# Layer norms with running moments, and four weight strips side by side, in a two-block transformer kernel on one NeuronCore

## What is computed

```
h = LN1(ALPHA*x + 0.5*swiglu(x))                       # FFN1, down projection, norm 1
h = LN2(ALPHA*h + token_mixers(h @ w_in) @ w_out)      # norm 2
h = LN3(ALPHA*h + cross_attention(h, LN(mem)))         # norm 3
h = LN4(ALPHA*h + 0.5*swiglu(h))                       # FFN2, down projection, norm 4
hm = rms_norm(h)*(1 + scale) + shift                   # "MODN": modulated input of block two
out = h + gate * merge(neighbourhood_attention(hm), short_conv(hm), conformer(hm))
_layer_norm(x): mu = mean(x); var = mean((x - mu)**2); (x - mu)*rsqrt(var + 1e-5)*g + b
```

## Time and profile before

| | us |
|---|---|
| median of 3 runs (lowest, highest) | 1776.18 (1774.76, 1776.67) |
| profiled execution, its own time | 1776.79 |
| its span | 1775.2 |
| TensorE busy | 1729.3 |
| VectorE busy | 964.0 |
| ScalarE busy | 678.1 |
| GpSimd busy | 167.3 |

### The profile page before, as it was taken

How to read it: one execution, slowest core, us unless ns; L and a number is a source line. 1 busy time by engine, 2 the same in 40 slices (tenths; PEclk the granted TensorE clock), 3 DMA queues, 4 the chain that set the end, 5 groups by cost and what they waited for, 6 DMA issues and landing times.

```text
span 1775.2 us, 22509 instructions
## 1 busy us (share of the span) xinstructions
PE 1729.3 (97%) x8312; PEld 1396.7 (79%) x8312; DVE 964.0 (54%) x1244; ACT 678.1 (38%) x945; POOL 167.3 (9%) x163
## 2 busy tenths in 40 slices
PE   8999999989999999999999999998999999999999
PEld 6888888857787778886888888865777777788887
DVE  4333339876964654546333333336968768744442
ACT  4232232244435455535322322235454544733321
POOL 0000001121013501012000000003010120000000
PEclk9999999999999999999999999998999999999999
DMA  5222247623222334122322323321222222133231
GB/s 207 95 95 95 95 139 244 210 70 126 73 72 75 104 131 154 60 83 72 106 95 99 101 95 107 107 83 54 84 94 92 88 86 83 59 127 111 100 104 69
DMA packets 50460, 183.74 MB, mean 104 GB/s; under 512 B 5664, under 2 KB 5920, under 8 KB 50016
## 3 DMA queue, kind: packets, MB, share of 16 engines
q1 hardware_dynamic: 44352, 161.50, 27.2%
q10 hardware_dynamic: 5040, 16.00, 2.6%
q0 software_dynamic: 1008, 5.41, 0.9%
HBM read 180.79 MB, written 2.10 MB: 103 GB/s over the span
## 4 chain that ended last, share of the span: by engine, by line
PE 89%; DVE 7%; ACT 2%; issue 1%; DMA 0%; DVEq 0%; ACTq 0%
PE proj L362 80%; PE aux L465 3%; DVE w_lo L354 1%; PE aux L1333 1%; DVE y L1487 1%; DVE a_lo L504 1%; PE aux L1320 1%; DVE h L500 1%; PE aux L1125 1%; ACT w_hi L347 1%; PE proj L1146 1%; PE aux L1310 0%; DVE score L764 0%; PE aux L1313 0%; DVE md L790 0%
## 5 line engine op out<-in xcount | busy, mean ns | idle before, releaser
L354 DVE TENSOR_TENSOR w_lo<-raw,w_hi 128x1024 fp32r<-128x1024 f32 x304 | 390.6, 1286 | 443.4 <-ACT w_hi L347 436.3
L362 PE MATMUL proj<-a_hi,w_hi 128*128 128x512 f32 x1504 | 598.3, 398 | 20.0 <-DVE a_lo L504 10.4
L362 PE MATMUL proj<-a_lo,w_hi 128*128 128x512 f32 x1504 | 589.1, 392 | 0.0
L362 PE MATMUL proj<-a_hi,w_lo 128*128 128x512 f32 x1504 | 589.1, 392 | 0.0
L347 ACT ACTIVATE w_hi<-raw 128x1024 fp32r<-128x1024 f32 x304 | 319.6, 1053 | 266.9 <-PE proj L362 243.3
L362 PEld LDWEIGHTS proj<-a_hi,w_hi 128*128 128x128 f32 x1504 | 284.5, 189 | 87.0 <-issue 26.2
L362 PEld LDWEIGHTS proj<-a_lo,w_hi 128*128 128x128 f32 x1504 | 284.6, 189 | 60.4 <-issue 2.6
L362 PEld LDWEIGHTS proj<-a_hi,w_lo 128*128 128x128 f32 x1504 | 284.3, 189 | 59.8
L362 PE MATMUL proj<-hid_hi,w_lo 128*128 128x512 f32 x352 | 137.1, 390 | 0.0
L362 PE MATMUL proj<-hid_lo,w_hi 128*128 128x512 f32 x352 | 137.1, 389 | 0.0
L362 PE MATMUL proj<-hid_hi,w_hi 128*128 128x512 f32 x352 | 137.1, 389 | 0.0
(11 more groups left out here) (296 smaller groups left out, 1941.3 us busy)
## 6 DMA issues: line engine op xcount, KB each, us to landing
raw<-stream SPq DMA_DIRECT2D x304, 512.0 KB, 3.5
ctxk<-ada_in ACTq DMA_DIRECT2D x12, 512.0 KB, 3.6
ctxv<-ada_in ACTq DMA_DIRECT2D x12, 512.0 KB, 4.2
h<-x_in SPq DMA_DIRECT2D x4, 512.0 KB, 6.9
out<-h ACTq DMA_DIRECT2D x8, 256.0 KB, 2.0
btab<-rpb_in POOLq DMA_DIRECT2D x4, 384.0 KB, 3.5
cond_row<-cond_in ACTq DMA_DIRECT2D x1, 1024.0 KB, 7.5
side<-mem_in POOLq DMA_DIRECT2D x1, 1024.0 KB, 5.1
```

Of the source, the lines that this page charges most:

```text
L354: nc.vector.tensor_tensor(w_lo[:, st.slot], raw[:, st.slot], w_hi[:, st.slot].bitcast(F32), ALU.subtract).then_inc(lo_ready, 1)
L362: mm = nc.tensor.matmul(dst, a, b, start=start and n == 0, stop=stop and n == 2)
```

## The change

Three things are edited.

First, norms 1, 3 and 4 get running moments. After the residual of chunk 4, TensorE makes the mean over the first four chunks (`pe_mid`, with a matrix of 1/512), and VectorE subtracts it from all 8 chunks (`dve_shift`), those not yet complete included. From then on ScalarE squares each complete chunk and VectorE adds the squares (`act_square`, `dve_add_square`) between the splits of the last strips. At the end four mean matmuls follow (`pe_moments`: sum, squares, last chunk, last square), ScalarE squares the mean, VectorE takes it from the mean square (`dve_variance`), and the remaining mean is subtracted chunk by chunk within `dve_normalise` (`dve_recentre`).

Second, norm 2 keeps its form, but VectorE adds its squares (`dve_add_squares`), so that one mean matmul stands where eight stood, and the order of splits around it is changed.

Third, `strip_quad` takes the place of `strip_pair` at the start of the mixer, of FFN2 and of the first round of the attention: four strips side by side for 5 of the 8 chunks, then each strip's last three chunks. The fourth strip's split is moved ahead for this. The loops over the residual projections of these norms are written out.

```
+        QUAD_BESIDE = 5
+        def strip_quad(pe, st, g, ready):
+            four = [(st.plus(j), g.plus(j)) for j in range(RING)]
+            for k in range(QUAD_BESIDE):
+                ready(k)
+                for s, gg in four:
+                    if k == 0:
+                        pe.wait_ge(lo_ready, s.n + 1)
+                        ge(pe, proj_read[gg.slot], gg.turn)
+                    product(proj[:, gg.slot], w_hi[:, s.slot, k * P:(k + 1) * P], w_lo[:, s.slot, k * P:(k + 1) * P],
+                            a_hi[:, k], a_lo[:, k], k == 0, False)
+            for s, gg in four:
+                for k in range(QUAD_BESIDE, KD):
+                    if s is four[0][0]:
+                        ready(k)
+                    mm = product(proj[:, gg.slot], w_hi[:, s.slot, k * P:(k + 1) * P],
+                                 w_lo[:, s.slot, k * P:(k + 1) * P], a_hi[:, k], a_lo[:, k], False, k == KD - 1)
+                mm.then_inc(strip_done, 1)
...
+        def residual_done(eng, m, c):
+            eng.wait_ge(proj_read[m.groups[c].slot], m.groups[c].turn + 1)
+        def pool_running(pool, m):
+            for c in (1, 2, 3):
+                residual_done(pool, m, c)
+                if c == 1:
+                    residual_done(pool, m, 0)
+                else:
+                    pool.wait_ge(r_sum, 5 * m.r + c - 1)
+                nc.gpsimd.tensor_tensor(zsum, h[:, 0] if c == 1 else zsum, h[:, c], ALU.add).then_inc(r_sum, 1)
+            pool.wait_ge(r_mid, m.r + 1)
+            for c in (5, 6):
+                residual_done(pool, m, c)
+                if c == 5:
+                    pool.wait_ge(r_shift, 8 * m.r + 5)
+                else:
+                    pool.wait_ge(r_sum, 5 * m.r + 4)
+                nc.gpsimd.tensor_tensor(zsum, h[:, 4] if c == 5 else zsum, h[:, c], ALU.add).then_inc(r_sum, 1)
+        def pe_mid(pe, m):
+            pe.wait_ge(r_sum, 5 * m.r + 3)
+            ge(pe, r_shift, 8 * m.r)
+            nc.tensor.matmul(aux[:, 2], mean_w[:], zsum, start=True, stop=True).then_inc(r_mid, 1)
+        def pe_moments(pe, m, beside=None):
+            pe.wait_ge(r_sum, 5 * m.r + 5)
+            ge(pe, r_cent, 8 * m.r)
+            nc.tensor.matmul(aux[:, 0], mean_d[:], zsum, start=True, stop=False)
+            pe.wait_ge(r_acc, 6 * m.r + 6)
+            nc.tensor.matmul(aux[:, 1], mean_d[:], rstd, start=True, stop=False)
+            if beside:
+                beside()
+            residual_done(pe, m, KD - 1)
+            nc.tensor.matmul(aux[:, 0], mean_d[:], h[:, KD - 1], start=False, stop=True).then_inc(r_mean, 1)
+            pe.wait_ge(r_sq, 9 * m.r + KD)
+            nc.tensor.matmul(aux[:, 1], mean_d[:], sq[:, 1], start=False, stop=True).then_inc(r_ms, 1)
+        def dve_shift(dve, m):
+            dve.wait_ge(r_mid, m.r + 1)
+            for c in range(KD):
+                if c == 4:
+                    residual_done(dve, m, 4)
+                nc.vector.tensor_tensor(h[:, c], h[:, c], aux[:, 2], ALU.subtract).then_inc(r_shift, 1)
+        def act_square(act, m, c):
+            if c == 0:
+                nc.scalar.preload_act_table_set(LN_EXP)
+            if c <= 4:
+                act.wait_ge(r_shift, 8 * m.r + c + 1)
+            else:
+                residual_done(act, m, c)
+            if c >= 2:
+                act.wait_ge(r_acc, 6 * m.r + max(1, c - 2))
+            nc.scalar.activation(sq[:, c % 2], h[:, c], ACT.Square).then_inc(r_sq, 1)
+        def dve_add_square(dve, m, c):
+            dve.wait_ge(r_sq, 9 * m.r + c + 1)
+            if c > 1:
+                dve.wait_ge(r_acc, 6 * m.r + c - 1)
+            nc.vector.tensor_tensor(rstd, sq[:, 0] if c == 1 else rstd, sq[:, c % 2], ALU.add).then_inc(r_acc, 1)
+        def dve_residual_of(dve, m, c, st, factor):
+            g = m.groups[c]
+            res = result(dve, st, g)
+            if c >= 5:
+                dve.wait_ge(r_shift, 8 * m.r + c + 1)
+            nc.vector.scalar_tensor_tensor(h[:, c], res, factor, h[:, c], ALU.mult,
+                                           ALU.add).then_inc(proj_read[g.slot], 1)
+        def dve_recentre(dve, m, c):
+            if c == KD - 1:
+                dve.wait_ge(r_sq, 9 * m.r + KD)
+            nc.vector.tensor_tensor(h[:, c], h[:, c], aux[:, 0], ALU.subtract).then_inc(r_cent, 1)
+        def act_mean_square(act, m):
+            act.wait_ge(r_mean, m.r + 1)
+            act.wait_ge(r_acc, 6 * m.r + 6)
+            nc.scalar.activation(sq[:, 0], aux[:, 0], ACT.Square).then_inc(r_sq, 1)
+        def act_running_std(act, m, chain):
+            act.wait_ge(r_var, m.r + 1)
+            inverse_root(chain, rstd, rstd, m.eps).then_inc(n_std, 1)
+        def dve_variance(dve, m, beside=None):
+            dve.wait_ge(r_sq, 9 * m.r + KD + 1)
+            dve.wait_ge(r_ms, m.r + 1)
+            nc.vector.tensor_tensor(rstd, aux[:, 1], sq[:, 0], ALU.subtract).then_inc(r_var, 1)
+            if beside:
+                beside()
+            dve_recentre(dve, m, 0)
+            dve_recentre(dve, m, 1)
...
+                    if m.r is not None:
+                        dve.wait_ge(r_cent, 8 * m.r + c + 1)
...
+                    if m.r is not None and c + 2 < KD:
+                        dve_recentre(dve, m, c + 2)
...
+        def dve_add_squares(dve, m, lo, hi):
+            for c in range(lo, hi):
+                dve.wait_ge(n_sq, m.q0 + c + 1)
+                if c > 1:
+                    dve.wait_ge(n_acc, m.a0 + c - 1)
+                nc.vector.tensor_tensor(rstd, sq[:, 0] if c == 1 else rstd, sq[:, c % 2], ALU.add).then_inc(n_acc, 1)
...
+        def pe_down(pe, s0, g0, hid0, m):
+            for c in range(KD):
+                for j in range(DOWN_STRIPS):
+                    if c == 0:
+                        pe.wait_ge(hid_l, hid0 + min(KF, SB * (j + 1)))
+                    feature_strip(pe, Nth(s0 + c * DOWN_STRIPS + j), Nth(g0 + c), hid_hi, hid_lo, first=SB * j,
+                                  blocks=min(SB, KF - SB * j), last=(j == DOWN_STRIPS - 1))
+                if c == 4:
+                    pe_mid(pe, m)
...
+        DOWN_SQUARES = {16: (0, 1), 17: (2, 3), 18: (4,), 19: (5,), 22: (6,)}
+        DOWN_ADDS = {17: (1,), 18: (2, 3), 19: (4,), 20: (5,), 23: (6,)}
+        XO_SQUARES = {5: (0, 1, 2, 3), 6: (4, 5), 7: (6,)}
+        XO_ADDS = {5: (1, 2), 6: (3, 4), 7: (5, 6)}
...
+        def dve_down(dve, s0, m, beside=None):
+            for a in range(DOWN_STRIPS * KD):
+                split_lo(dve, Nth(s0 + a + 3))
+                if beside:
+                    beside(a)
+                for c in DOWN_ADDS.get(a, ()):
+                    dve_add_square(dve, m, c)
+                c, j = a // DOWN_STRIPS, a % DOWN_STRIPS
+                if j == DOWN_STRIPS - 1:
+                    dve_residual_of(dve, m, c, Nth(s0 + a), 0.5 / ALPHA)
+                    if c == 4:
+                        dve_shift(dve, m)
...
+            act_squares(act, LN2, hi=6)
+            act_memkv(act, 0, 2)
+            act_squares(act, LN2, lo=6)
+            act_memkv(act, 2, 5)
...
+                split_hi(act, Nth(S_XO + n + 3))
+                for c in XO_SQUARES.get(n, ()):
+                    act_square(act, LN3, c)
+            act_only_splits(act, S_CTXV, 0, 1)
+            act_square(act, LN3, KD - 1)
+            act_mean_square(act, LN3)
+            act_only_splits(act, S_CTXV, 1, 2)
+            act_running_std(act, LN3, chain)
+            act_hi(act, LN3, 0, 2)
+            act_only_splits(act, S_CTXV, 2, 3)
+            act_hi(act, LN3, 2, 3)
+            act_only_splits(act, S_CTXV, 3, 4)
             act_ctxv_take(act)
-            act_hi(act, LN3)
-            act_ffn(act, S_FFN2, G_FFN2)
-            act_splits(act, S_DOWN2, DOWN_STRIPS * KD)
-            act_squares(act, LN4)
-            act_std(act, LN4, chain)
+            act_hi(act, LN3, 3, 5)
+            split_hi(act, Nth(S_FFN2 + 3))
+            act_hi(act, LN3, 5)
...
+            dve_variance(dve, LN1, lambda: split_lo(dve, Nth(S_MIX + 3)))
...
-            dve_centre(dve, LN2)
-            dve_only_splits(dve, S_MEMK, 1, 3)
-            dve_only_splits(dve, S_MEMK, 3, 6)
+            dve_centre(dve, LN2, 0, 4)
+            dve_add_squares(dve, LN2, 1, 2)
+            dve_centre(dve, LN2, 4, 6)
+            dve_add_squares(dve, LN2, 2, 3)
+            dve_centre(dve, LN2, 6, 8)
+            dve_add_squares(dve, LN2, 3, 6)
+            dve_only_splits(dve, S_MEMK, 1, 2)
+            dve_add_squares(dve, LN2, 6, 8)
+            dve_only_splits(dve, S_MEMK, 2, 6)
...
-            dve_residual(dve, S_XO, G_XO, 1.0 / ALPHA, before=LN2)
-            dve_centre(dve, LN3)
-            dve_only_splits(dve, S_CTXV, 0, 2)
-            dve_only_splits(dve, S_CTXV, 2, 4)
-            dve_normalise(dve, LN3)
-            dve_ffn(dve, S_FFN2, G_FFN2, KF)
-            dve_residual(dve, S_DOWN2, G_DOWN2, 0.5 / ALPHA, DOWN_STRIPS, before=LN3)
-            dve_centre(dve, LN4)
```

(95 more changed lines are left out.)

142 lines of the change are left out of this document (68 added, 74 removed).

## The result

| | us |
|---|---|
| changed kernel, median of 5 runs | 1762.52 |
| kernel before, median of 5 runs beside it | 1775.96 |
| ratio, 95% interval | 0.9928 (0.9915 to 0.994) |
| predicted | 1768.0 (1762 to 1773) |
| profiled execution of the change, its own time and span | 1761.14, 1759.5 |

The change makes the kernel 13.4 us faster, where 8.1 were forecast. One of the five executions took 4946.63 us: in it a matmul of a product lasted 925 ns instead of 397.

What follows compares the result with a forecast made beforehand. The prediction took TensorE, busy 1729.3 of 1775.2 us, to bound the kernel. Its terms, -4.0 - 4.7 + 0.6 + 0 = -8.1 us, took the median 1776.18 to 1768.1, given as 1768.0, range 1762 to 1773.

Steps and rivals of the forecast that it cites:

- Norm 1: From norm 1 to the mixer's fifth strip: running moments and quad bring -4.0 us, bounds -1.5 to -5.
- its sign of being right: At norm 1, the first `a_lo` comes about 12 us after the last product instead of 15.6.
- the rival built on it: Slower (5%): in the first down projection, 18 VectorE products take 2.32 us each beside GpSimd; +12 us, 1788.
- the half clock: After TensorE's idle stretch at norm 1, the slow start of the quad costs 1.7 us as before, or 2.5.
- Norm 2: At norm 2, the first normalising starts earlier, by -4.7 us; bounds -2.5 and -6.7.
- the ring: At norm 2, normalising, `a_hi`, `w_hi` and `w_lo` wait for one another, 7 rounds of 3.65 us; TensorE doesn't end the stage.
- Norm 3: From norm 3 to FFN2's fifth strip: +0.6 us, bounds -3 and +3.
- Both waits: In the first chunk of FFN2's quad, TensorE waits twice for `w_lo`, 3 and 5 us; 8.4 us lost where 2.66 were.
- Norm 4 and the attention: From norm 4 through the attention: the quad's fifth strip starts 5.5 us earlier, but the gain is 0; bounds +1.5 and -5.5.
- `glu` comes no earlier: At the attention, `glu` needs strips 0 and 1; the quad ends strip 0 at 1229.5, the pair at 1229.6.
- The reasoning on VectorE's chain: In the attention, the chain ending last runs through VectorE, from `glu` through the taps, busy 11.61 of 12 us.
- the attention keeps its 5.5: Rival (12%): at the attention the 5.5 us are kept, as TensorE's own waits there are short; -13.6 us, 1762.6.

Runs made afterwards that it cites:

- experiment 5: Changed kernel, all three quads kept, one norm put back as before: norm 4 undone 1768.53 us, norm 1 undone 1766.24 us.
- experiment 2: Changed kernel with a pair of strips instead of the quad at one place: at the attention alone 1758.59 us, at FFN2 alone 1759.48 us.
- experiment 3: Kernel before with only norm 2 changed (squares added on VectorE, one mean matmul, new order of splits): 1770.75 us, ratio 0.9972.
- experiment 6: GpSimd's loads of band and first bias table moved ahead of norm 4's shifts: changed kernel, quads kept, 1761.56 us; kernel with two pairs (FFN2, attention) 1753.77 us.

## Why the prediction was right in direction and short in size

**Norm 1 (-4.0, measured -4.9 in this trace, -4.2 to -4.8 in seven others; moments alone 3.3 to 4.1 by experiment 5).** The mechanism held link by link: it is 10.7 us from the mean matmul to the quad (10.8 by the prediction's own steps, though its sign of being right says "about 12"), and VectorE ended the last residual 2.0 us after the mean matmul, when it was reckoned to. So its load of shifting and adding is paid for by free time, and the rival built on it is out. What was too dear is the half clock: granted clock 0.50 and then 0.90, which cost 1.4 us here and 1.4 to 2.0 in the others, not 1.7 to 2.5, as the windows (busy by engine, granted clock, DMA) show:

```profile
381.00:383.00 2.00, 2.00 (x6) 1.52 (x6) 2.00 (x4) 0.72 (x1) 1.21 (x2) 0.50 0.00 0
383.00:385.00 2.00, 2.00 (x10) 1.60 (x9) 2.00 (x5) 0.73 (x1) 1.21 (x2) 0.90 0.00 0
```

**Norm 2 (-4.7, measured -4.8 to -5.1).** Right: the first normalising came 24.75 us after the mean matmul, 24.86 by the prediction's own steps. Seven matmuls of 0.96 us left TensorE, and the time followed the ring.

**Norm 3 (+0.6, measured -1.0; in three other profiles -0.3 to 0.0).** Both waits are there. The first ended 18.5 us after the projection (19.2 reckoned), the second after 24.2 instead of 25.2, for the most part because VectorE made each chunk in 1.92 us and not in the 1.92 + 0.4 for GpSimd that the prediction granted. Half clock behind the second wait cost 1.4 us in this execution and 2.2 to 2.5 in the other three, where 1.7 to 2.5 were reckoned; that is most of what separates them. Against before, the stage with a pair is 3.1 us shorter (experiment 2), so the moments bring that much, and the quad takes nearly all of it back.

**Norm 4 and the attention (0, measured -3.7; in three other profiles -2.8 to -3.1).** This is the term that was mis-sized: "`glu` comes no earlier", and so nothing is gained. The first normalising gained 6.0 us (5.6 taken), in every profile alike. How much of it reaches strip 0 is not settled: here strip 0 was taken 2.0 us nearer (0.1 reckoned), but 0.8 of that is the eight mean matmuls, which took 9.71 us instead of the 10.51 of the earlier trace rows and scatter from 9.5 to 10.7 over the twelve profiles, in either code:

```profile
1197.85 9.66 PE L465 MATMUL aux<-sq,mean_d 128*128 128x512 f32 x16 [3.47 <-ACT sq L485]
```

```profile
1184.10 10.52 PE L491 MATMUL aux<-sq,mean_d 128*128 128x512 f32 x16 [4.30 <-ACT sq L609]
```

The first of these rows is the old code (experiment 3), the second the new (quads with the early loads). Over the two profiles with the old code and the four with the new, strip 0 comes between 0.4 later and 2.1 nearer. Half clock behind the quad's start cost 1.8 in all four, not 2.4. What no step had, and what every profile shows, is the second part: with the quad `glu` starts only after GpSimd's six additions have ended, where it stood beside them before. From the start of `w_lo` to that of the first tap it is 3.64 and 3.66 us in the two profiles with the old code, 3.4 to 3.6 with a pair and the late loads, and 2.14 in all five with the quad at the attention; with the first tap itself, some 1.7 us of contention went. The reasoning on VectorE's chain was right: the gain passed through it, and TensorE waited 3.5 us before the scores (the row of L1438), until VectorE had made their `nq` behind the taps, at 1238.71 + 0.74. With the pair strip 0 is taken 4.5 us earlier (34.5 us after the stage's mean matmul against 39.0), and against the kernel before the stage keeps 6.3 to 6.6 us in the four profiles with the pair and the late loads. The rival "the attention keeps its 5.5" names almost the measured time, 1762.6, but not its origin, which is luck: with the quad the stage kept 2.8 to 3.7, and 0.8 less of it against experiment 3's execution of the old code.

**Sum.** In the profiled execution the errors are -0.9, -0.3, -1.6 and -3.7, all of one sign, and -1.1 of its start, which is scatter. The changed kernel with the early loads (experiment 6) has nearly the same span, 1759.7, by another route: the stages of norms 3 and 4 are each 0.8 us longer, and a stretch of half clock within the mixer, which the profile of the kernel before shows and which costs 1.6 us here (last section), is missing there. It is missing in eight of the nine profiles with the quad at the mixer, and the prediction had no term for it. So the forecast was short, by the traces, by the contention at the attention (1.7) and, in most executions, by this stretch of the mixer; the rest is parts under 1 us each, which one profile can't size.

## What to carry over

In these runs four strips side by side paid at the mixer, where VectorE's pace for a chunk (1.92 us) lies between that of a pair (1.36) and of four (2.73), where all four splits were ready at the start, and where nobody waited for the first strip alone. They lost at FFN2, where the splits came late, and at the attention, where strip 0 was waited for. Where the chain that sets the end runs through VectorE, look at what GpSimd does beside it: additions that nobody waits for cost 1.7 us there, and earlier loads removed that. A term of zero whose parts are each a few us and cancel is not a safe zero: it needs its own range for each part. And a stage's gain under 1 us should be read from several executions, of both kernels, before a cause is given to it.
